# First chunk of a hybrid decoder step: the recurrence-side mixing placed beside the last gates, six half gate units placed behind the first scores, the recurrence placed earlier

## Chip, cores and metric

One core of one Trainium2 chip runs the whole step. The metric is the device time of one execution in microseconds; for a kernel the median of its runs is given.

## What is computed

One layer of a hybrid decoder works on 1024 prompt tokens and 8 sample tokens, with a model width of 1024, in 32-bit floats. The part that matters here, cut from the reference:

```python
proj = rmsnorm(x, norm_mix) @ w_in
u_s5, x_lru, y_lru, g_a, g_b = split(proj)
a_out = s5_branch(u_s5, ...)             # state scan, then z * sigmoid(z @ w_glu + b)
b_out = rglru_branch(x_lru, y_lru, ...)  # conv, gates, scan, times gelu(y_lru)
merged = sigmoid(g_a) * (a_out @ w_proj_a) + sigmoid(g_b) * (b_out @ w_proj_b)
x = x + merged @ w_out
x = x + peer(rmsnorm(x, norm_ffn), w_q, sub_keys, u_tab, v_tab)
```

In `peer`, each token ranks keys for 8 heads and takes the 16 best experts of each. An expert is one row of `u_tab` and one of `v_tab`, so 128 expert rows are gathered for every token, 1024 + 1024 numbers each.

## The kernel before

The prompt is cut into four chunks of 256 tokens, and a chunk into two tiles of 128. The sample tokens ride with the last chunk. Each chunk has a trunk (input projections, state scan, recurrence, gates, mixing, output) and an expert part: for every list position of a tile one gather brings 128 rows, one for each token, 1 MB with both tables. VectorE takes the dot product of the u half with the normed token (line 1824, `dots`), ScalarE turns it into a weight (line 856 is its helper), and TensorE adds the v half, weighted by a diagonal matrix (line 2277, `values`). GpSimd issues the gathers (line 802, `gather`). The trunk of a later chunk runs between the batches of the chunk ahead of it, by due times (`paced`, line 357). The first chunk has no expert work to run beside, so its trunk stands alone, and it is written out by hand so that the first tile's first list is ready soon: `first_lists` on TensorE (line 2345), VectorE (line 1942) and ScalarE (line 990).

In the trunk of the first chunk TensorE goes through units of eight products; a unit has 128 output channels and 256 tokens. Line 2165 is `project`, and a matmul in 32 bits stands as two records in the trace, so a unit is x16. Behind the four recurrence gates come gate units 4 to 15 (`U_GATE` + m). Between them stand the state steps: `s5_in` (line 2182) and `s5_out` (line 2206, with the skip part at line 2194 for every second one). How many of the sixteen steps are done ahead of gate unit m is fixed in a tuple, and the steps are in the order input 0, input 1, output 0, input 2, output 1 and so on:

```python
FIRST_AFTER = (1, 1, 2, 4, 6, 8, 8, 10, 12, 12, 12, 14, 14, 15, 15, 16)
```

So output 3 and input 5 stand ahead of gate unit 7, output 4 and input 6 ahead of unit 8, and output 7 ahead of unit 15. Output j waits for the three VectorE pieces of state pair j (`s5`, line 1559; a scan is line 1581, the last copy of a pair line 1606). Input j + 1 waits for the first two products of pair j, which read PSUM. VectorE's order of pieces is a string: S is a state piece, L is half of one of the four recurrence units (`lru`, line 1609; scan at line 1619); a C does nothing in the first chunk:

```python
FIRST_DVE = "SSSSSCSCSCSCSSSSSS" + "SL" * 8 + "SS"
```

In `first_lists`, TensorE then does the gated unit of the state branch for tile 0 (line 2366), the eight mixing units of tile 0 (line 2321, `mix_side`: four products for side 0, the state branch, and four for side 1, the recurrence), its output (line 2388), transposes (line 2360), the first head's queries (line 2353) and scores (line 2412). While VectorE ranks the first list (`first_topk`, line 1696), TensorE does what is left of the gated units of tile 1, spreads the norm's weights over a bank (line 2243), and begins the mixing of tile 1. This goes on when VectorE has finished the last gated products, in `last_gates`. Behind it come the second head's queries and scores, the output of tile 1 (line 2435) with the first batches of `values` between its units, and the other heads.

VectorE follows: the mixing of a unit takes three operations (`mix`, line 1916), then the residual (line 1314), then the norm. `first_topk` releases the first eight gathers through `best_ok` and the next eight through `idx_ok`. In `upto(OLD + k)` the first k batches of two dots are done. One such batch stands in the middle of tile 1's mixing, two more stand inside the second ranking, and two more between that ranking and the residual of tile 1.

Gathers go round five pairs of cells (15 cells of 4 KB a partition; `u_cell`, `v_cell`), so gather i waits for the dot of row i - 5, and for the v product of row i - 10. Weights come through a ring of two slots that hold a pair of units, or have a home of their own (`HOMES`, line 89): output weights, five mixing weights, the gated units' weights, and three mixing weights parked in cells 13, 14 and 12. A gather that would write a cell in use waits for the units that read it (lines 834 to 839). SyncE loads in the order of use, and waits for a ring slot (`slot_free`, line 682) or, ahead of the output weights, for the recurrence (`lru_ok`). At position 68 of that order it waits for the end of tile 1's mixing, then loads keys and query weights; the next chunk's columns wait for the residual of tile 1.

Of the kernel before, what the change touches and what calls it, by code (L numbers as in the profile page):

```python
# [14 lines left out]
P = 128  # L15
# [53 lines left out]
U_MIX0, U_OUT0, U_Q0, U_MIX1, U_Q01, U_OUT1, U_Q1, UNITS0 = 36, 44, 52, 54, 62, 64, 72, 88  # L69
SLOTS0 = UNITS0 - 4  # L70
TRUNK = 28
EVACS0 = 56
# [15 lines left out]
MIX_CELLS = (13, 14, 12)  # L88
HOMES = RESIDENT + GLU_W + MIX_PARKED
# [31 lines left out]
FIRST_DVE = "SSSSSCSCSCSCSSSSSS" + "SL" * 8 + "SS"  # L121
# [204 lines left out]
def slot_unit(c, l):  # L326

    if c:
        return l if l < L_GATE else l + 8
    return l if l < U_GATE else ga_unit(c, l - U_GATE) if l < TRUNK else l + 4  # L330
# [61 lines left out]
def build(nc, i_, o_):  # L392

    with ExitStack() as ctx:
# [5 lines left out]
        def sem(name):  # L400
# [101 lines left out]
        assert W.at <= T.at + GLU_AT and min(MIX_CELLS) * D >= GLU_AT + QT * DB  # L502
        homes = [R.take(D) for _ in RESIDENT] \
            + [rows_[:, GLU_AT + DB * k:GLU_AT + DB * k + DB] for k in range(QT)] \
            + [cells[:, k] for k in MIX_CELLS]
# [157 lines left out]
        def _(sp):  # L663
# [58 lines left out]
            def first_chunk():  # L722

                for l in range(2 * RING, SLOTS0):
                    if l == 68:
                        sp.wait_ge(unit, U_MIX1 + KT)
                        keys(1, 0)
                    if l == 72:
                        next_columns(0)
                    if l >= 72 and l % 4 == 0:  # L730
                        pair = (l - 64) // 4
                        keys(pair, 2 * (pair - 1) if pair > 2 else 0)
                    if l == U_OUT0 - 4:
                        sp.wait_ge(lru_ok, QT)
                    slot_free(0, l)
                    load_weights(0, l)
                    if l == 47:
                        load_x(0, False)
                        sp.wait_ge(y_mm, SJ // 2)
                        sp.dma_start(kb0, i_["keys"][:, 0:4, :]).then_inc(key0_in, 16)  # L740
# [42 lines left out]
        def _(pool):  # L783
# [39 lines left out]
            def gathers(c, first, last):  # L823

                for i in range(first, last):
# [8 lines left out]
                    if c == 0 and i < UV:  # L834
                        held = {u_cell(i), v_cell(i)}
                        if held & {GLU_AT // D, GLU_AT // D + 1}:
                            pool.wait_ge(glu_mm, 2 * QT)
                        if held & set(MIX_CELLS):
                            pool.wait_ge(unit, U_MIX1 + 1 + max(k for k, cell in enumerate(MIX_CELLS) if cell in held))
                    gather_to(place(c, i), flat(idxn)[:, i:i + 1])  # L840
# [13 lines left out]
        def _(act):  # L854
# [135 lines left out]
            def first_lists(upto):  # L990
# [45 lines left out]
                root(0, 0)  # L1036
                for h, first_unit in enumerate((U_Q0, U_Q01)):
                    if h:
                        for q in range(2, QT):
                            glu(q, QT + q, slice(P, C))  # L1040
                        soft(0, P, 1)
                    for s in range(2):
                        query(first_unit + s, h, s, qT0[:, s])
# [34 lines left out]
            def chunk(c, last):  # L1078
# [56 lines left out]
                def mixing_gate(m):  # L1135
# [7 lines left out]
                    af(dst, PB[u % 2][:, 0:n], ACT.Tanh, scale=0.5).then_inc(evac, 1)  # L1143
# [158 lines left out]
        def _(dve):  # L1302
# [639 lines left out]
            def first_lists(upto):  # L1942
# [31 lines left out]
                for m in range(KT):  # L1974
                    mix(0, m, U_MIX0 + m, early, MIXB[m % 2])
# [16 lines left out]
                scale(0)  # L1992
                for i, m in enumerate(LAST_FIRST):
                    if i == QT:
                        upto(OLD + 1)
                    mix(0, m, U_MIX1 + 4 * (i // 4) + 3, late, [b[:, P * (i % 4):P * (i % 4) + P] for b in MIXB[i // 4]])
                dve.wait_ge(s_ev, 2)
                for piece, _ in enumerate(topk(1, P, 1, lambda t: gn[:, 1], lambda t: idxn[:, 1])):
                    if piece == 1:
                        upto(OLD + 2)  # L2000
                    elif piece == 3:
                        upto(OLD + 3)
# [127 lines left out]
        def _(pe):  # L2130
# [214 lines left out]
            def first_lists(upto):  # L2345

                def query(u, s, cols, evicted):

                    w = slot(0, u - 4)
# [22 lines left out]
                pe.wait_ge(lru_ok, QT)  # L2372
                pe.wait_ge(glu_ev, QT)
                w01 = [slot(0, TRUNK + QT + m) for m in range(2)]
                for m in range(2):
                    mix_side(w01[m], 1, MIXB[m], early)
                pe.wait_ge(a0_ok, QT)
                for m in range(2):
                    mix_side(w01[m], 0, MIXB[m], early).then_inc(unit, 1)
                for m in range(2, KT):  # L2380
                    pe.wait_ge(mix_ok, m - 1)
                    mix(0, TRUNK + QT + m, MIXB[m % 2], early)
# [23 lines left out]
                def head(h, first_unit):  # L2406

                    for s in range(2):
                        query(first_unit + s, s, early, U_MIX0 + 2 * h)
                    pe.wait_ge(evac, U_MIX0 + 2 * h + 2)  # L2410
# [14 lines left out]
                for i in range(KT):  # L2425
                    if i >= QT:
# [4 lines left out]
                for i, k in enumerate(LAST_FIRST):  # L2431
                    pe.wait_ge(mix_ok, KT + i + 1)
                    w = slot(0, U_OUT1 - 4 + k)
# [15 lines left out]
                for h in range(2, HEADS):  # L2449
                    for s in range(2):  # L2450
                        upto(at0_proj(h, s))
                        query(U_Q1 + 2 * (h - 2) + s, s, slice(0, C), U_MIX0 + 2 * h + s - 1)
# [3 lines left out]
                    pe.wait_ge(evac, U_MIX0 + 2 * h + 2)  # L2456
# [10 lines left out]
                for h in range(2):  # L2467
                    for s in range(2):
                        upto(at0_proj(HEADS, 0) + 2 * h + s)
                        query(U_Q1 + 12 + 2 * h + s, s, late, U_MIX0 + 16 + 2 * h + s - 1)  # L2470
# [11 lines left out]
            def chunk(c, last):  # L2482
# [33 lines left out]
                if first:  # L2516
# [201 lines left out]
```

## Time and profile before

| what | value |
|---|---|
| median of 3 runs | 3051.58 us (3050.4 to 3053.53) |
| the profiled execution: time | 3053.22 us |
| the profiled execution: span | 3051.4 us |
| mean granted TensorE clock | 0.866 |
| DMA traffic | 1215.48 MB, 398 GB/s over the span |
| busy share of the span: TensorE, VectorE, ScalarE, GpSimd | 80%, 71%, 40%, 37% |

The span runs from the first to the last instruction of the profiled execution; its time has the launch around it. The shares of the engines are means over stages with different limits: in the first 190 us the gathers have not begun, and in the rest they run all the time. PE is TensorE, DVE VectorE, ACT ScalarE, POOL GpSimd, SP SyncE. A row of a timeline has the start, the length, and in brackets the idle time ahead of it with what ended it.

### The profile page before, as it was taken

What the parts mean: (1) busy time and instruction counts of PE and PEld (TensorE: products, weight loads), DVE (VectorE), ACT (ScalarE), POOL (GpSimd) and SP (SyncE); (2) the same over time, 40 slices, a digit from 0 to 9 for tenths busy, and PEclk for the clock granted to TensorE, in tenths of its full rate; (3) what the DMA queues carried; (4) which work ended last, traced back from release to release, by engine and by line L of the source; (5) the groups of instructions that cost most, each with busy time, mean ns of one, the idle gap of its engine ahead of it and who ended that gap; (6) DMA issues with size and microseconds to landing.
All of it is one profiled execution on the core that took longest, in us unless ns stands there. A gap on an engine that the chain in (4) does not pass through costs nothing.

```text
span 3051.4 us, 43432 instructions
## 1 busy us (share of the span) xinstructions
PE 2442.7 (80%) x14628; PEld 1180.5 (39%) x14628; DVE 2162.8 (71%) x5374; ACT 1207.0 (40%) x3786; POOL 1121.5 (37%) x1048
## 2 busy tenths in 40 slices
PE   9997768899887778899877768888977776766776
PEld 7863324565343324455233324455433321111111
DVE  7757887776479876676468987676558897554445
ACT  2224444433345444333335444433244444333333
POOL 0023443433334443333333443333334444433332
PEclk9998888999988879999988879999988886677667
DMA  4569999999999999999999999999999999999998
GB/s 156 200 242 408 407 411 421 420 417 414 412 420 412 421 420 420 421 404 421 420 421 406 406 419 413 421 419 420 419 414 419 409 416 419 419 421 421 420 421 344
DMA packets 176079, 1215.48 MB, mean 398 GB/s; under 512 B 22360, under 2 KB 22744, under 8 KB 31472
## 3 DMA queue, kind: packets, MB, share of 16 engines
q0 software_dynamic: 148608, 1082.20, 85.9%
q1 hardware_dynamic: 25744, 126.19, 10.4%
q10 hardware_dynamic: 1504, 4.33, 0.4%
q8 instruction: 115, 1.88, 0.3%
q14 instruction: 108, 0.88, 0.1%
HBM read 1208.12 MB, written 4.51 MB: 397 GB/s over the span
## 4 chain that ended last, share of the span: by engine, by line
DMA 29%; issue 22%; PE 20%; DVE 15%; POOL 11%; ACT 2%; DVEq 0%; ACTq 0%; POOLq 0%; SPq 0%
DMA arena<-in_uv,arena 15%; DMA arena<-in_vu,arena 14%; POOL arena L802 11%; PE psum L2277 7%; DVE arena L1824 6%; PE psum L2165 5%; PE psum L2321 3%; DVE arena L1306 3%; ACT arena L856 2%; DVE arena L1314 1%; DVE arena L1687 1%; PE psum L2341 1%; PE psum L2353 1%; DVE arena L1645 1%; DVE arena L1310 0%
## 5 line engine op out<-in xcount | busy, mean ns | idle before, releaser
L1824 DVE CUSTOM_DVE_ANT_0 arena<-arena 128x1024 f32<-128x1024 f32 x1024 | 1246.7, 1224 | 762.5 <-DMA arena<-in_uv,arena 392.4
L2277 PE MATMUL psum<-arena 64*64 64x512 f32 x8184 | 1282.6, 730 | 556.2 <-ACT arena L856 504.4
L856 ACT ACTIVATE arena<-arena 128x1 f32<-128x1 f32 (+3 forms) x3252 | 932.6, 289 | 1630.8 <-DVE arena L1824 1449.6
L802 POOL DMA_INDIRECT arena<-in_vu,arena x517 | 554.5, 1073 | 987.8 <-DVE arena L1824 690.7
L802 POOL DMA_INDIRECT arena<-in_uv,arena x515 | 563.8, 1095 | 920.6 <-DVE arena L1824 810.5
L2277 PEld LDWEIGHTS psum<-arena 64*64 64x64 f32 x8184 | 276.1, 150 | 1370.2 <-ACT arena L856 1102.9
L2165 PE MATMUL psum<-arena 128*128 128x256 f32 (+1 forms) x2656 | 653.7, 403 | 2.8 <-DVE arena L1314 1.7
L2165 PEld LDWEIGHTS psum<-arena 128*128 128x128 f32 x2656 | 519.3, 200 | 201.9 <-issue 122.7
L1306 DVE TENSOR_TENSOR arena<-arena 128x256 f32<-128x256 f32 (+11 forms) x562 | 249.9, 471 | 12.9 <-ACT psum L856 0.8
L856 ACT ACT_TABLE_LOAD x119 | 152.7, 1283 | 10.9 <-DVE arena L1306 7.0
L856 ACT ACTIVATE arena<-psum 128x256 f32<-128x256 f32 (+5 forms) x246 | 95.2, 400 | 108.9 <-PE psum L2165 79.6
L2321 PE MATMUL psum<-arena 128*128 128x128 f32 (+2 forms) x640 | 119.1, 343 | 2.3 <-DVE arena L1314 1.7
L1314 DVE SCALAR_TENSOR_TENSOR arena<-arena 128x256 f32<-128x256 f32 (+8 forms) x287 | 98.1, 354 | 20.6 <-ACT arena L856 15.2
L2321 PEld LDWEIGHTS psum<-arena 128*128 128x128 f32 x640 | 100.0, 191 | 28.5 <-issue 11.2
L2341 PE MATMUL psum<-arena 128*128 128x512 f32 x192 | 88.7, 604 | 0.0
L1824 DVE DVE_READ_ACCUMULATOR2_ANT arena<- 128x1 f32 x1024 | 84.3, 82 | 0.0
L1314 DVE SCALAR_TENSOR_TENSOR arena<-arena,psum 128x128 f32<-128x128 f32 (+4 forms) x101 | 51.2, 544 | 27.0 <-PE psum L2321 21.9
L1581 DVE TENSOR_TENSOR_SCAN arena<-arena 128x64 f32<-128x64 f32 x256 | 68.9, 332 | 1.3
L2353 PE MATMUL psum<-arena 128*128 128x256 f32 (+1 forms) x320 | 64.0, 357 | 0.4 <-issue 0.4
L2353 PEld LDWEIGHTS psum<-arena 128*128 128x128 f32 x320 | 53.3, 202 | 22.8 <-issue 17.9
L1306 DVE TENSOR_TENSOR arena<-psum,arena 128x512 f32<-128x512 f32 (+2 forms) x91 | 59.7, 685 | 1.3 <-PE psum L2277 0.2
L856 ACT ACTIVATE arena<-psum,arena 128x256 f32<-128x256 f32 (+3 forms) x75 | 31.5, 450 | 70.7 <-PE psum L2360 31.2
(139 smaller groups left out, 1048.0 us busy)
## 6 DMA issues: line engine op xcount, KB each, us to landing
arena<-in_w_in SPq DMA_DIRECT2D x56, 1024.0 KB, 9.1
arena<-in_w_q SPq DMA_DIRECT2D x34, 1024.0 KB, 9.6
arena<-in_vu,arena POOLq DMA_INDIRECT x517, 11.3
arena<-in_uv,arena POOLq DMA_INDIRECT x515, 11.3
arena<-in_w_ab SPq DMA_DIRECT2D x11, 512.0 KB, 10.0
arena<-in_keys SPq DMA_DIRECT2D x17, 256.0 KB, 7.7
arena<-in_w_out SPq DMA_DIRECT2D x8, 512.0 KB, 16.0
arena<-in_x_tok SPq DMA_DIRECT2D x8, 512.0 KB
```

The source lines that it names most:

```text
L802: pool.indirect_dma_start(rows_[:, first:first + 2 * D], None, table, bass.IndirectOffsetOnAxis(column, 0)).then_inc(uv_in[at % UV], 16)
L856: return nc.scalar.activation(out, in_, f, **kw)
L1306: return V.tensor_tensor(out, a, b, op)
L1314: return V.scalar_tensor_tensor(out=out, in0=a, scalar=s1, in1=b, op0=op0, op1=op1)
L1581: return V.tensor_tensor_scan(v, mag2[:, j:j + 1].to_broadcast([P, SEG]), v, start, ALU.mult, ALU.add)
L1645: ins = V.match_replace(M[:, k], SV[:, k, best], src[:, k], NEG)
L1824: V.tensor_tensor_reduce(out=u, in0=u, in1=hn, scale=1.0, scalar=0.0, op0=ALU.mult, op1=ALU.add, accum_out=dots_[:, b % DOTS, k:k + 1]).th ...
L2165: ins = mm(PB[u % 2][:, 0:n], w[:, P * t:P * t + P], rhs[:, t, 0:n], start=(t == 0), stop=(t == k - 1))
L2277: ins = mm(PV[o:o + HP, half], dg[r:r + HP, PAIR * (b % 2) + k], cells[r:r + HP, v_cell(place(c, i)), at:at + 512], start=(i % (SLOT // 2) ...
L2321: ins = mm(banks[side][:, 0:cols.stop - cols.start], w[:, 512 * side + P * t:512 * side + P * t + P], src[:, t, cols], start=(t == 0), sto ...
L2341: ins = mm(OUTB[t][half][0:rn], hT[c][:, k, r0:r0 + rn], w[:, 512 * half:512 * half + 512], start=(k == 0), stop=(k == KT - 1))
L2353: ins = mm(PB[s][:, 0:n], w[:, P * t:P * t + P], gb[:, t, cols], start=(t == 0), stop=(t == KT - 1))
```

## The change

Six of the twelve later gate units, numbers 10 to 15, are computed for the first tile alone in the trunk. Their second tile's half comes later, behind the first head's scores, in two banks by turns, and ScalarE evicts it (`late_gate`): two ahead of the first softmax, four behind it. For this the six weights get homes in cells 9, 10, 12, 13, 2 and 5, the parked mixing weights move to cells 14, 11 and 8, and gathers into these cells wait for the late units. The load into cell 2 waits for the state tables that used the place.

The recurrence side of tile 0's eight mixing units goes beside gate units 12 to 15, two units at each, into the two banks called `x2T`; in `first_lists` only the state side is left, into four banks by turns. So TensorE waits for the whole recurrence ahead of the first of them, at gate unit 12, and VectorE's order of pieces has each recurrence unit in one go, the last behind the fourteenth state piece. The two halves of tile 1's mixing swap their banks. VectorE does the first two batches of dots ahead of tile 1's mixing, and none within it. `FIRST_AFTER` stays. The core of the diff:

```diff
...
-U_MIX0, U_OUT0, U_Q0, U_MIX1, U_Q01, U_OUT1, U_Q1, UNITS0 = 36, 44, 52, 54, 62, 64, 72, 88
-SLOTS0 = UNITS0 - 4
+LATE_GATES = (10, 11, 12, 13, 14, 15)
+LATE = len(LATE_GATES)
+U_MIX0, U_OUT0, U_Q0, U_LATE = 36, 44, 52, 54
+U_MIX1, U_Q01, U_OUT1, U_Q1, UNITS0 = (u + LATE for u in (54, 62, 64, 72, 88))
+SLOTS0 = UNITS0 - 4 - LATE
...
-MIX_CELLS = (13, 14, 12)
-HOMES = RESIDENT + GLU_W + MIX_PARKED
+MIX_CELLS = (14, 11, 8)
+LATE_W = tuple(("w_in", U_GATE + m) for m in LATE_GATES)
+LATE_CELLS = (9, 10, 12, 13, 2, 5)
+HOMES = RESIDENT + GLU_W + MIX_PARKED + LATE_W
...
-FIRST_DVE = "SSSSSCSCSCSCSSSSSS" + "SL" * 8 + "SS"
+FIRST_DVE = "S" * 10 + "SLL" * 4 + "S" * 10
...
+                    if weight(0, l) == LATE_W[4]:
+                        sp.wait_ge(s5_ok, 1)
...
+                        elif held & set(LATE_CELLS):
+                            pool.wait_ge(unit, U_LATE + 1 + max(k for k, cell in enumerate(LATE_CELLS) if cell in held))
...
+                def late_gate(i):
+                    act.wait_ge(unit, U_LATE + i + 1)
+                    af(gb[:, LATE_GATES[i] % KT, P:C], SB[i % 2][:, 0:P], ACT.Tanh, scale=0.5).then_inc(evac, 1)
+
...
+                        for i in range(2):
+                            late_gate(i)
...
+                        for i in range(2, LATE):
+                            late_gate(i)
...
-                    af(dst, PB[u % 2][:, 0:n], ACT.Tanh, scale=0.5).then_inc(evac, 1)
+                    k = P if first and m in LATE_GATES else n
+                    af(dst[:, 0:k], PB[u % 2][:, 0:k], ACT.Tanh, scale=0.5).then_inc(evac, 1)
...
-                    mix(0, m, U_MIX0 + m, early, MIXB[m % 2])
+                    mix(0, m, U_MIX0 + m, early, (GLUB[m % 4], x2T[:, P * m:P * m + P]))
...
+                dve.wait_ge(hn_ok, 1)
+                upto(OLD + 2)
+                dve.wait_ge(evac, U_MIX0 + 2 + LATE)
...
-                    if i == QT:
-                        upto(OLD + 1)
-                    mix(0, m, U_MIX1 + 4 * (i // 4) + 3, late, [b[:, P * (i % 4):P * (i % 4) + P] for b in MIXB[i // 4]])
+                    mix(0, m, U_MIX1 + 4 * (i // 4) + 3, late, [b[:, P * (i % 4):P * (i % 4) + P] for b in MIXB[1 - i // 4]])
...
-                        upto(OLD + 2)
+                        upto(OLD + 3)
...
-                        upto(OLD + 3)
+                        upto(OLD + 4)
...
-                pe.wait_ge(lru_ok, QT)
...
-                w01 = [slot(0, TRUNK + QT + m) for m in range(2)]
-                for m in range(2):
-                    mix_side(w01[m], 1, MIXB[m], early)
...
-                for m in range(2):
-                    mix_side(w01[m], 0, MIXB[m], early).then_inc(unit, 1)
-                for m in range(2, KT):
-                    pe.wait_ge(mix_ok, m - 1)
-                    mix(0, TRUNK + QT + m, MIXB[m % 2], early)
+                for m in range(KT):
+                    if m >= QT:
+                        pe.wait_ge(mix_ok, m - QT + 1)
+                    mix_side(slot(0, TRUNK + QT + m), 0, (GLUB[m % 4], None), early).then_inc(unit, 1)
...
+                pe.wait_ge(glu_ev, QT + 2)
+                for i, m in enumerate(LATE_GATES):
+                    w = slot(0, U_GATE + m)
+                    if i >= 2:
+                        pe.wait_ge(evac, U_MIX0 + 1 + i)
+                    for t in range(KT):
+                        ins = mm(SB[i % 2][:, 0:P], w[:, P * t:P * t + P], hT[0][:, t, late], start=(t == 0), stop=(t == KT - 1))
+                    ins.then_inc(unit, 1)
...
-                places = [[b[:, P * (i % 4):P * (i % 4) + P] for b in MIXB[i // 4]] for i in range(KT)]
-                w1 = [slot(0, U_MIX1 - 4 + m) for m in LAST_FIRST]
+                places = [[b[:, P * (i % 4):P * (i % 4) + P] for b in MIXB[1 - i // 4]] for i in range(KT)]
+                w1 = [slot(0, U_MIX1 - 4 - LATE + m) for m in LAST_FIRST]
...
+                    if i == QT:
+                        pe.wait_ge(evac, U_MIX0 + 2 + LATE)
...
-                        project(c, ga_unit(c, m), U_GATE + m, hT[c], KT, n)
+                        project(c, ga_unit(c, m), U_GATE + m, hT[c], KT, P if m in LATE_GATES else n)
+                        if m >= EARLY_SIDES:
+                            if m == EARLY_SIDES:
+                                pe.wait_ge(lru_ok, QT)
+                            for k in range(2 * (m - EARLY_SIDES), 2 * (m - EARLY_SIDES) + 2):
+                                mix_side(slot(c, TRUNK + QT + k), 1, (None, x2T[:, P * k:P * k + P]), slice(0, P))
...
```

What is left out of the diff renumbers units, evictions and waits by the six new units, and gives the new cells their place in the list of homes.

## Rows read from the trace of the kernel before

**Rows 1.** The page: gigabytes a second in 40 equal slices, and the gather queue.

```profile
GB/s 156 200 242 408 407 411 421 420 417 414 412 420 412 421 420 420 421 404 421 420 421 406 406 419 413 421 419 420 419 414 419 409 416 419 419 421 421 420 421 344
q0 software_dynamic: 148608, 1082.20, 85.9%
```

**Rows 2.** Windows by stage: us, busy by engine, granted clock, DMA share, GB/s.

```profile
90.00:189.00 99.00, 96.28 (x671) 79.73 (x668) 59.67 (x204) 17.30 (x40) 0.32 (x1) 1.00 0.46 173
190.00:230.00 40.00, 38.33 (x242) 23.25 (x244) 30.35 (x90) 14.62 (x42) 15.63 (x14) 1.00 0.99 401
230.00:265.00 35.00, 29.25 (x172) 16.72 (x164) 23.84 (x78) 17.66 (x48) 11.06 (x10) 0.91 1.01 419
265.00:280.00 15.00, 12.90 (x68) 6.21 (x69) 14.69 (x45) 6.19 (x21) 7.56 (x6) 0.74 0.95 360
```

**Rows 3.** Timeline of GpSimd, gathers 1, 5 and 16: start us, us, what.

```profile
188.68 1.09 POOL L802 DMA_INDIRECT arena<-in_vu,arena  x1 [184.83 <-DVEq L1752]
193.86 0.94 POOL L802 DMA_INDIRECT arena<-in_vu,arena  x1 [0.30 <-issue]
232.14 1.68 POOL L802 DMA_INDIRECT arena<-in_uv,arena  x1 [4.84 <-DVE arena L1824]
```

**Rows 4.** Chain of waits on TensorE to the first gather: start us, us, what.

```profile
98.50 1.00 PE psum L2206 x16
99.50 1.09 PE psum L2182 x16
100.59 3.65 PE psum L2165 x16
104.24 0.57 PE psum L2194 x16
106.90 10.56 PE psum L2165 x48
...
147.86 10.99 PE psum L2321 x96
```

**Rows 5.** Timeline of VectorE, state pieces and the first recurrence unit.

```profile
96.06 1.28 DVE L1306 TENSOR_TENSOR arena<-psum,arena 128x512 f32<-128x512 f32 x2
...
103.21 0.76 DVE L1314 SCALAR_TENSOR_TENSOR arena<-arena 128x256 f32<-128x256 f32 x2
103.88 1.28 DVE L1306 TENSOR_TENSOR arena<-psum,arena 128x512 f32<-128x512 f32 x2
...
105.88 0.42 DVE L1314 SCALAR_TENSOR_TENSOR arena<-arena 128x256 f32<-128x256 f32 x1
...
107.52 1.07 DVE L1581 TENSOR_TENSOR_SCAN arena<-arena 128x64 f32<-128x64 f32 x4
```

**Rows 6.** TensorE's timeline and windows of 1 us where its clock fell and rose.

```profile
259.86 3.69 PE L2277 MATMUL psum<-arena 64*64 64x512 f32 x16 [3.83 <-ACT arena L856]
300.19 3.51 PE L2277 MATMUL psum<-arena 64*64 64x512 f32 x16 [2.13 <-ACT arena L856]
...
259.00:260.00 1.00, 0.14 (x4) 0.14 (x8) 1.00 (x4) 0.70 (x4) 0.94 (x1) 0.51 0.96 401
303.00:304.00 1.00, 1.00 (x10) 0.35 (x3) 0.81 (x2) 0.00 (x0) 0.00 (x0) 0.80 1.06 442
```

**Rows 7.** Timeline of TensorE behind the first head's scores.

```profile
183.95 3.74 PE L2321 MATMUL psum<-arena 128*128 128x128 f32 x32
189.42 10.98 PE L2321 MATMUL psum<-arena 128*128 128x128 f32 x96 [1.74 <-DVE arena L1314]
```

**Rows 8.** Timelines of VectorE (residual, eleventh row's dot, third ranking) and ScalarE (its scores).

```profile
226.45 1.29 DVE L1314 SCALAR_TENSOR_TENSOR arena<-psum,arena 128x512 f32<-128x512 f32 x2 [0.66 <-PE psum L2435]
230.64 1.23 DVE L1824 CUSTOM_DVE_ANT_0 arena<-arena 128x1024 f32<-128x1024 f32 x1 [0.16 <-issue]
251.23 0.87 DVE L1642 MAX8 arena<-arena 128x8 f32<-128x128 f32 x4
...
244.79 0.82 ACT L856 ACTIVATE arena<-psum,arena 128x256 f32<-128x256 f32 x2
```

More of the change, by code:

```diff
@@ L67 @@
 EVACS = 56
-U_MIX0, U_OUT0, U_Q0, U_MIX1, U_Q01, U_OUT1, U_Q1, UNITS0 = 36, 44, 52, 54, 62, 64, 72, 88
-SLOTS0 = UNITS0 - 4
+LATE_GATES = (10, 11, 12, 13, 14, 15)
[3 more added lines that the diff above has]
+SLOTS0 = UNITS0 - 4 - LATE
 TRUNK = 28
-EVACS0 = 56
+EVACS0 = 56 + LATE
+EARLY_SIDES = 2 * KT - KT // 2
 LAST_FIRST = (5, 6, 7, 0, 1, 2, 3, 4)
@@ L329, in slot_unit @@
         return l if l < L_GATE else l + 8
-    return l if l < U_GATE else ga_unit(c, l - U_GATE) if l < TRUNK else l + 4
+    return l if l < U_GATE else ga_unit(c, l - U_GATE) if l < TRUNK else l + 4 if l < U_LATE - 4 else l + 4 + LATE
 def columns(c):
@@ L501, in build @@
         GLU_AT = 6 * D
-        assert W.at <= T.at + GLU_AT and min(MIX_CELLS) * D >= GLU_AT + QT * DB
+        assert W.at <= T.at + GLU_AT and min(MIX_CELLS + LATE_CELLS[:4]) * D >= GLU_AT + QT * DB
         homes = [R.take(D) for _ in RESIDENT] \
             + [rows_[:, GLU_AT + DB * k:GLU_AT + DB * k + DB] for k in range(QT)] \
-            + [cells[:, k] for k in MIX_CELLS]
+            + [cells[:, k] for k in MIX_CELLS + LATE_CELLS]
         dg = R.take(2 * PAIR, HP)
@@ L2347, in query @@
                 def query(u, s, cols, evicted):
-                    w = slot(0, u - 4)
+                    w = slot(0, u - 4 if u < U_LATE else u - 4 - LATE)
                     pe.wait_ge(evac, evicted)
@@ L2406, in head @@
                 def head(h, first_unit):
+                    evicted = U_MIX0 + (2 + LATE) * h
                     for s in range(2):
-                        query(first_unit + s, s, early, U_MIX0 + 2 * h)
-                    pe.wait_ge(evac, U_MIX0 + 2 * h + 2)
+                        query(first_unit + s, s, early, evicted)
+                    pe.wait_ge(evac, evicted + 2)
                     for s in range(2):
@@ L2432, in first_lists @@
                     pe.wait_ge(mix_ok, KT + i + 1)
-                    w = slot(0, U_OUT1 - 4 + k)
+                    w = slot(0, U_OUT1 - 4 - LATE + k)
                     for half in range(2):
@@ L2451, in first_lists @@
                         upto(at0_proj(h, s))
-                        query(U_Q1 + 2 * (h - 2) + s, s, slice(0, C), U_MIX0 + 2 * h + s - 1)
+                        query(U_Q1 + 2 * (h - 2) + s, s, slice(0, C), U_MIX0 + LATE + 2 * h + s - 1)
                     if h == 5:
@@ L2455, in first_lists @@
                     upto(at0_scores(h))
-                    pe.wait_ge(evac, U_MIX0 + 2 * h + 2)
+                    pe.wait_ge(evac, U_MIX0 + LATE + 2 * h + 2)
                     pe.wait_ge(key_in[h // 2 % 2], 16 * ((h // 2 - 1) // 2 + 1))
@@ L2469, in first_lists @@
                         upto(at0_proj(HEADS, 0) + 2 * h + s)
-                        query(U_Q1 + 12 + 2 * h + s, s, late, U_MIX0 + 16 + 2 * h + s - 1)
+                        query(U_Q1 + 12 + 2 * h + s, s, late, U_MIX0 + LATE + 16 + 2 * h + s - 1)
                 upto(at0_scores(HEADS))
```

## Prediction, made before the changed kernel was run

> **What bounds the kernel.** I read the page's slices first. From the fourth slice on, the DMA engines move about 420 GB/s to the end, and one queue, the gathers of expert rows, carries 1082 MB of it [rows 1]. The windows by stage say the same: 173 GB/s before the first gather, 419 behind it [rows 2]. So the end is set by three things: when the stream of gathers starts, how many bytes follow, and where the stream runs dry. The bytes stay the same here. Everything this change does is in the first 270 us, and it counts only if it moves the first gather, issued at 188.68 [rows 3], or makes a hole behind it.
>
> In the chain of waits, TensorE leads to the first gather: it is busy for 96 of 99 us at full clock [rows 2], through gate units, state steps, the first tile's mixing and its output [rows 4]. VectorE is as full over the state pieces: from 96.06 to 107.52 its rows follow one another without a gap [rows 5]. That second engine is what one must not lose sight of.
>
> **Shorter gates (removed from the path).** A gate unit of 256 columns takes 10.56/3 = 3.52 on TensorE; eight products of 128 columns, with their weights, take 10.99/6 = 1.83, the time of a mixing unit [rows 4]. Six units cut to their first tile give 6 x 1.69 = 10.1 us.
>
> **The recurrence side of the first mixing (moved).** 32 products leave the stage behind the gates and come in beside the last four gates; by the same row that is 7.3 us out and 7.3 us in, so nothing. The mixing stage keeps the other 7.3 us. What it loses in waits is nothing either, since TensorE had none there.
>
> **The recurrence (moved up).** The order of VectorE becomes ten state pieces, then four times one piece and a whole recurrence unit (two halves), then ten pieces. A unit costs 103.21 to 103.88 and 105.88 to 107.52 [rows 5], 0.67 + 1.64 = 2.31. Back to back, the second half also waits for the first half's writes, which a state piece hides today; between 0 and 0.2 us, I take 0.04, so 2.35. The work is the same, but every state piece behind is late by the units ahead of it until the units are done, and TensorE's program keeps its fixed places for the state steps. Step by step: state output 3, at 98.50 [rows 4], needs the piece that ended as the next began, at 96.06 [rows 5]; one unit later is 98.41. No wait. State input 5, at 99.50 [rows 4], needs the first products of the next piece, ready at 97.34 [rows 5], two units later: 102.04. Wait 2.5. The input's 1.09 and a gate's 3.65 and 0.57 [rows 4] bring TensorE to 107.4. State output 4 needs the piece that ended as the recurrence began, at 103.21 [rows 5], now behind four units: 112.6. Wait 5.2. State input 6 needs 1.28 more of VectorE [rows 5] while the output takes 1.00 [rows 4]: wait 0.3.
>
> So the three gates that began at 106.90 [rows 4] begin 8.0 us later. From there VectorE runs unbroken again and TensorE is behind it, so no wait is left. A small wait for the gated branch, today hidden partly by the recurrence side, grows by some 0.3 us.
>
> **The clock.** A wait of 3.83 on TensorE was followed by a granted clock of 0.51, that is 1.2 instead of 2.4 GHz; after work began at 300.19 the clock was back late in the window from 303, which reads 0.80 [rows 6]. A wait of 1.74 left it at 1.00 [rows 2, 7]. The 5.2 here is longer than the first, so I count 3.2 us of work at half clock: 1.6 lost, between 0 (the clock stays) and 2.6 (as long at half clock as the wait itself). The Trainium skill, "TensorE: Matmul & The Clock Gate", Part 1, says that the throttled state is the default and that activity releases it. By that rule read strictly the wait of 2.5 would cost its 1.6 as well, and the first gather would come at +1.4; by the row that kept its clock over 1.74 it comes at -0.2.
>
> Sum to the first gather: -10.1 + 8.0 + 0.3 + 1.6 = -0.2, bounds -1.8 and +0.8. Ten microseconds of saved work are mostly spent in waiting for pieces that the recurrence has pushed back.
>
> **Weights kept for later.** Six half-megabyte loads go to cells of their own instead of the ring, so the queue of SyncE passes them earlier, with the mixing and output weights behind them; the wait on the state tables is long over at that point. The load windows before the first gather are half empty (DMA share 0.46 [rows 2]). Cost nothing; if that cover went, a late mixing weight would stop TensorE. On GpSimd's queue the fourth and fifth gathers now wait for late units. By the sums below these end at 187.6 and 191.3, and the fifth gather goes out at 193.86 [rows 3], everything behind it later still. Nothing.
>
> **The six second halves (added behind the first scores).** Today TensorE has from 183.95 a recurrence side of 3.74 us, then 1.74 us of waiting, then 10.98 us of second-tile mixing, to 200.4 [rows 7]. Now 6 x 1.83 = 11.0 us come in ahead and swallow the wait: 9.2 us later, 209.6. ScalarE's six short evictions stand beside the first ranking, four of them queued behind its softmax, which itself now stands behind the first two; TensorE's fifth half waits for the third eviction, which follows the softmax and is over by then. If the softmax came late, the second tile would be late with it, by as much. From here on TensorE is without a break up to the second tile's output, so the residual, at 226.45, and the dot that waits behind it on VectorE, at 230.64 [rows 8], both come 9.2 us later, whatever the four dots moved ahead of the mixing bring: the program has the same ten dots before that residual as today.
>
> A gather can start only when the dot of the row five before it is done. So the sixteenth gather goes from 232.14 [rows 3] to 241.3. Would the queues be dry by then? By shapes, fifteen rows (1.05 MB each), two pairs of query weights, the next columns (1.05 MB each) and two key blocks (0.26) are 19.4 MB. From 190 to 230, 401 GB/s moved 16.0 [rows 2]; the other 3.4 MB last 8.0 us, to 238.0. A gather's data moves 1.3 to 3 us behind its issue (188.68, and 1.7 us missing in that window against 419 GB/s); I take 2. Slack: 238.0 - 2 - 232.14 = 3.9. A hole of 9.2 - 3.9 = 5.3 us.
>
> Some comes back. The third ranking, at 251.23, stands behind its rows today, not behind its scores; these are out at 245.61 [rows 8], 254.8 after. VectorE is then 3.6 late, the stream 5.3, and from 265 to 280 the stream is short of dots today (share 0.95, 360 GB/s [rows 2]). Between 0 and 1.7 us; I take 1.0.
>
> **Sum.** -0.2 + 5.3 - 1.0 = +4.1 us. The profiled execution has a span of 3051.4 and a time of 3053.22, 1.6 above the median; its time would be 3057.3, and the median 3051.58 becomes 3055.7. 0.2%, about what a measurement here can tell from no change, is 6.1 us: the forecast is no change, on the slow side.
>
> **Rivals.** First, slower: the hole takes the whole delay. At the second tile's residual, VectorE waits for TensorE with its rows landed. If the early dots let the stream eat its backlog sooner, or smaller holes open between the dots inside the second ranking, then all 9.2 us are dry, with the start at its worst, +0.8: +10.0, 3061.6. It decides once the backlog at the sixteenth gather is below 3.9 us. For it: only nine rows can be asked for before the second ranking begins. Against: the weight loads, also late, fill in between. 0.22.
>
> Second, a little faster: the clock stays and the ramp is covered. That is -1.8 and a hole of nothing: 3049.8. For it: four dots come ahead of the mixing and ask for four rows sooner, and the late weight loads fill in. Against: the count of bytes, in which both already stand. 0.14.
>
> Third, faster: the change does what its words say and TensorE does not wait for the state pieces. Then the first gather comes 9.8 earlier, the ramp's 4.3 stays: -5.5, 3046.1. It needs state steps that are not due at those places; the chain shows TensorE arriving at output 3 with 2.4 to spare and no more. 0.06.
>
> **How the numbers follow.** The forecast has 0.58; its own range is 3051.5 to 3060, from the bounds of clock, hole and return. The range 3048.8 to 3062 takes in the second rival and the slower one's middle. Slower by over 0.2%: nearly all of the first rival and about an eighth of the forecast, 0.28. Faster: over half of the last rival and a little for what I have not seen, 0.05. Same: 0.67.
>
> **What would show it.** In the changed trace: the recurrence's last write near 110; TensorE idle by 2.5 and 5.2 us before state input 5 and output 4; a granted clock below 1 near 113 to 118; the first mixing's end near 159; the first gather between 187 and 190; the second tile's mixing ending 9 us later against the first gather; a dip of DMA in the windows near 236 to 243. The forecast is wrong if the first gather comes before 185, or if the DMA share stays at 1.00 through 245, or if the sixteenth gather is less than 6 us later.

## The result, and the profile after

The median of 19 runs is 3057.88 us, against 3051.58 for 19 runs of the kernel before beside them. The ratio is 1.0017 with a 95% interval of [1.0011, 1.0024], so the kernel is 5.2 us slower (0.0017 x 3051.58), between 3.4 and 7.3. The medians lie 6.3 apart and the means 5.3, since the runs of after spread over 7.8 us and those of before over 3.8. By the 0.2% of the prediction (6.1 us) this is no change, on the slow side, though the upper end of the interval lies above it. The profiled execution of after took 3058.52 with a span of 3056.7. Its span is 5.3 above the one of before, 3051.4.

The page of after, gigabytes a second in 40 slices and the gather queue:

```profile
GB/s 155 237 191 388 415 413 415 421 416 414 416 421 412 413 420 421 421 409 421 420 420 409 412 420 405 421 420 420 418 415 417 403 420 420 420 421 422 421 420 344
q0 software_dynamic: 148608, 1082.20, 85.7%
```

Packets and bytes are those of [rows 1]. The third and fourth slices are thinner, 191 for 242 and 388 for 408; from there on the two kernels look alike. So the difference was made in the first 310 us. Windows by stage (busy time by engine, granted clock, DMA share, GB/s):

```profile
90.00:189.00 99.00, 91.14 (x676) 76.23 (x672) 59.25 (x198) 16.96 (x40) 0.00 (x0) 0.95 0.45 173
190.00:230.00 40.00, 38.33 (x276) 29.70 (x275) 28.24 (x88) 12.69 (x38) 13.45 (x13) 1.00 0.94 368
230.00:265.00 35.00, 34.53 (x203) 18.88 (x201) 20.51 (x64) 15.12 (x45) 11.27 (x10) 1.00 0.95 362
265.00:280.00 15.00, 9.61 (x55) 4.33 (x52) 14.61 (x40) 8.33 (x25) 6.51 (x5) 0.77 1.01 416
```

Against [rows 2], TensorE is busy for 91 instead of 96 of the 99 us before the first gather, at a mean clock of 0.95. From 190 to 265 the stream moved 14.7 + 12.7 = 27.4 MB where before it moved 16.0 + 14.7 = 30.7: 3.3 MB less, 7.9 us at 419 GB/s. From 265 to 280 it is the other way: 416 for 360 GB/s, 0.84 MB or 2.0 us given back.

Gathers 1, 6, 15 and 16 on GpSimd's timeline (start us, us, what, idle before):

```profile
190.28 1.09 POOL L810 DMA_INDIRECT arena<-in_vu,arena  x1 [186.43 <-DVEq L1771]
...
198.28 0.94 POOL L810 DMA_INDIRECT arena<-in_uv,arena  x1 [1.89 <-DVE arena L1843]
...
234.99 0.94 POOL L810 DMA_INDIRECT arena<-in_vu,arena  x1 [2.75 <-PE psum L2297]
242.46 1.68 POOL L810 DMA_INDIRECT arena<-in_uv,arena  x1 [6.53 <-DVE arena L1843]
```

Against [rows 3] the start is 1.6 late and the sixteenth gather 10.3, so 8.7 us of delay were added between them. TensorE's timeline shows both parts:

```profile
98.83 1.07 PE L2226 MATMUL psum<-arena 128*32 128x128 f32 x16
102.46 1.17 PE L2202 MATMUL psum<-arena 32*128 32x128 f32 x16 [2.56 <-DVE arena L1325]
103.56 5.35 PE L2185 MATMUL psum<-arena 128*128 128x256 f32 x16
...
113.05 1.33 PE L2226 MATMUL psum<-arena 128*32 128x128 f32 x16 [3.57 <-DVE arena L1625]
114.31 2.08 PE L2202 MATMUL psum<-arena 32*128 32x128 f32 x16
116.31 11.03 PE L2185 MATMUL psum<-arena 128*128 128x256 f32 x48
...
153.07 7.38 PE L2341 MATMUL psum<-arena 128*128 128x128 f32 x64 [0.83 <-ACT arena L866]
160.29 13.90 PE L2403 MATMUL psum<-arena 128*128 128x512 f32 x32
...
185.55 10.88 PE L2441 MATMUL psum<-arena 128*128 128x128 f32 x96
196.27 14.46 PE L2341 MATMUL psum<-arena 128*128 128x128 f32 x128
```

State input 5 waits 2.56 us for VectorE and state output 4 another 3.57; gate unit 7 between them takes 5.35 instead of 3.65 [rows 4]. Near the end stand the six late halves, 10.88 us, and behind them the second tile's mixing without a break. Why unit 7 is slow, the windows of 1 us say (the clock is the third number from the end):

```profile
103.00:104.00 1.00, 1.00 (x13) 0.87 (x10) 0.97 (x4) 0.00 (x0) 0.00 (x0) 0.74 1.03 414
104.00:105.00 1.00, 1.00 (x3) 0.73 (x3) 0.96 (x2) 0.00 (x0) 0.00 (x0) 0.50 1.02 414
...
106.00:107.00 1.00, 1.00 (x4) 0.81 (x3) 0.93 (x6) 0.00 (x0) 0.00 (x0) 0.56 1.02 418
107.00:108.00 1.00, 1.00 (x6) 0.88 (x5) 0.96 (x6) 0.00 (x0) 0.00 (x0) 1.00 1.01 412
...
114.00:115.00 1.00, 1.00 (x10) 0.70 (x8) 0.94 (x3) 0.00 (x0) 0.00 (x0) 0.50 1.01 401
...
120.00:121.00 1.00, 1.00 (x5) 0.86 (x4) 1.00 (x3) 0.00 (x0) 0.00 (x0) 0.73 1.05 418
```

The granted clock fell to 0.50 (1.2 GHz) behind each of the two waits and came back to 1.00 within the windows from 106 and from 120. VectorE, from the last recurrence unit to the third ranking:

```profile
108.21 1.20 DVE L1333 SCALAR_TENSOR_TENSOR arena<-arena 128x256 f32<-128x256 f32 x3
...
112.83 0.17 DVE L1625 COPY arena<-arena 128x4 f32<-128x4 f32 x1
...
236.77 1.29 DVE L1333 SCALAR_TENSOR_TENSOR arena<-psum,arena 128x512 f32<-128x512 f32 x2 [5.33 <-PE psum L2461]
240.96 1.23 DVE L1843 CUSTOM_DVE_ANT_0 arena<-arena 128x1024 f32<-128x1024 f32 x1 [0.16 <-issue]
...
256.91 1.23 DVE L1843 CUSTOM_DVE_ANT_0 arena<-arena 128x1024 f32<-128x1024 f32 x1 [2.49 <-DMA arena<-in_uv,arena]
258.06 0.87 DVE L1661 MAX8 arena<-arena 128x8 f32<-128x128 f32 x4
```

The copy at 112.83 ends the piece that state output 4 wants. The residual and the eleventh dot are 10.3 late against [rows 8], with VectorE idle for 5.33 ahead of the residual. The dot at 256.91 waits for its row, and the third ranking stands right behind it, 6.8 late.

### The profile page after: what moved, and what is told of

The parts are those of the page before. It is cut to its first block, busy times and chain, and to the rows that moved or that the text cites. A ratio compares the mean times of both kernels' runs of the same rounds, so it can differ in the third digit from the quotient of the medians.

```text
span 3056.7 us, 43640 instructions
## 1 busy us (share of the span) xinstructions
PE 2432.9 (80%) x14724; PEld 1173.2 (38%) x14724; DVE 2162.7 (71%) x5374; ACT 1206.8 (39%) x3792; POOL 1125.1 (37%) x1048
## 4 chain that ended last, share of the span: by engine, by line
DMA 31%; issue 21%; PE 20%; DVE 14%; POOL 10%; ACT 3%; ACTq 0%; DVEq 0%; POOLq 0%; SPq 0%
DMA arena<-in_uv,arena 17%; DMA arena<-in_vu,arena 14%; POOL arena L810 10%; PE psum L2297 9%; DVE arena L1843 6%; PE psum L2185 4%; DVE arena L1325 3%; PE psum L2341 3%; ACT arena L866 2%; DVE arena L1333 1%; PE psum L2361 1%; DVE arena L1706 1%; DVE arena L1600 1%; PE psum L2373 0%; PE psum L2403 0%
## 5 line engine op out<-in xcount | busy, mean ns | idle before, releaser
L2185 PE MATMUL psum<-arena 128*128 128x256 f32 (+2 forms) x2656 | 636.4, 396 | 3.7 <-DVE arena L1333 1.8
L2185 PEld LDWEIGHTS psum<-arena 128*128 128x128 f32 x2656 | 507.2, 198 | 198.2 <-issue 122.5
L2341 PEld LDWEIGHTS psum<-arena 128*128 128x128 f32 x640 | 100.1, 190 | 26.7 <-issue 13.0
L2373 PE MATMUL psum<-arena 128*128 128x256 f32 (+1 forms) x320 | 61.0, 345 | 0.4 <-issue 0.4
L2373 PEld LDWEIGHTS psum<-arena 128*128 128x128 f32 x320 | 50.8, 193 | 21.5 <-issue 17.1
L2361 PEld LDWEIGHTS psum<-arena 128*128 128x128 f32 x192 | 36.0, 197 | 56.8 <-issue 56.8
```

The lines of the kernel that those rows point to most:

```text
L2185: ins = mm(PB[u % 2][:, 0:n], w[:, P * t:P * t + P], rhs[:, t, 0:n], start=(t == 0), stop=(t == k - 1))
L2341: ins = mm(banks[side][:, 0:cols.stop - cols.start], w[:, 512 * side + P * t:512 * side + P * t + P], src[:, t, cols], start=(t == 0), sto ...
L2361: ins = mm(OUTB[t][half][0:rn], hT[c][:, k, r0:r0 + rn], w[:, 512 * half:512 * half + 512], start=(k == 0), stop=(k == KT - 1))
L2373: ins = mm(PB[s][:, 0:n], w[:, P * t:P * t + P], gb[:, t, cols], start=(t == 0), stop=(t == KT - 1))
```

## The experiments

All eight are edits of the changed kernel, in two groups on two chips (e1 to e4, e5 to e8), each with its own runs of the kernel before beside it (median 3052.14 of 33 runs for the first group, 3052.47 of 21 for the second). The ratios are taken against these, so between groups the ratios and the gathers can be compared, and the medians can't. The time differences in the text are these ratios applied to 3051.58; where two edits are compared, it is by their ratios.

| kernel | first gather | sixteenth gather | median us | ratio to before [95%] |
|---|---|---|---|---|
| before | 188.68 | 232.14 | 3051.58 | 1 |
| after | 190.28 | 242.46 | 3057.88 | 1.0017 [1.0011, 1.0024] |
| e1_steps | 179.51 | 231.70 | 3048.39 | 0.9985 [0.9976, 0.9994] |
| e2_filler | 186.90 | 239.10 | 3054.56 | 1.0008 [0.9999, 1.0017] |
| e3_dots | 190.12 | 236.09 | 3055.99 | 1.0012 [1.0003, 1.0021] |
| e4_order | 187.23 | 239.42 | 3056.14 | 1.0013 [1.0004, 1.0022] |
| e5_steps_dots | 179.66 | 225.63 | 3045.08 | 0.9976 [0.9966, 0.9986] |
| e6_steps_whole | 198.78 | 242.25 | 3061.92 | 1.0030 [1.0018, 1.0042] |
| e7_steps_three | 186.41 | 233.24 | 3049.36 | 0.9988 [0.9979, 0.9997] |
| e8_old_dots | 190.58 | 242.77 | 3062.24 | 1.0033 [1.0020, 1.0045] |

**e1_steps: the state steps put where VectorE can serve them.** Each entry of the tuple says how many of the sixteen steps are done ahead of a gate unit; lower entries are later steps. The last step goes behind the gates.

```diff
-FIRST_AFTER = (1, 1, 2, 4, 6, 8, 8, 10, 12, 12, 12, 14, 14, 15, 15, 16)
+FIRST_AFTER = (1, 1, 2, 4, 6, 8, 8, 9, 10, 10, 10, 12, 12, 14, 14, 15)
...
-                if not first:
+                if first:
+                    first_s5(2 * (SJ // 2))
+                else:
                     s5_until(AT_GLU)
```

> The changed kernel with the state steps that TensorE waits for issued later among the gate units (input 5 behind gate unit 7, output 4 and input 6 behind unit 10, the last output behind unit 15). My theory: the early recurrence costs only because these steps keep their places. TensorE then has no wait above 1 us between 98 and 150, its clock stays at 1.00, the first mixing ends near 149 and the first gather goes out near 179 instead of 190.3; the hole behind it stays, so the time is some 10 us below the changed kernel: about 3047 us, 3044 to 3050. Rival, that VectorE's state pieces bound the stage whatever TensorE's order: the first gather stays at 187 or later and the time above 3054.

TensorE's timeline, from state output 3 on:

```profile
98.47 1.07 PE L2226 MATMUL psum<-arena 128*32 128x128 f32 x16
99.47 3.72 PE L2185 MATMUL psum<-arena 128*128 128x256 f32 x16
103.11 1.16 PE L2202 MATMUL psum<-arena 32*128 32x128 f32 x16
104.20 8.96 PE L2185 MATMUL psum<-arena 128*128 128x256 f32 x48
...
149.53 10.90 PE L2403 MATMUL psum<-arena 128*128 128x512 f32 x25
```

A gate unit now stands where the wait of 2.56 was, and the three units that took 11.03 take 8.96. The first mixing ends at 149.53 instead of 160.29, where the output begins (this view ends at 160, so its last row is cut short). The first gather goes out at 179.51, 9.2 earlier than before the change and 10.8 earlier than after it. So the waits came from the fixed places of the steps, and the saving of 10.1 us of gates is real once they go; VectorE was not the bound. The time is 9.8 below after, as expected. Against before it falls by 4.6, though, half of the 9.2: the sixteenth gather is only 0.4 earlier than before, so 8.7 of the 9.2 are gone there, as in after, and part of them comes back later.

**e2_filler: idle products in the two waits.** The waits stay; products of ones into a bank that nobody reads keep TensorE busy in them.

```diff
+                if c == 0 and jp == 5:
+                    for _ in range(5):
+                        mm(PV[:, 1, 0:C], ones, ones[:, 0:1].to_broadcast([P, C]), start=True, stop=True)
...
+                if c == 0 and jp == 4:
+                    for _ in range(11):
+                        mm(PV[:, 1, 0:C], ones, ones[:, 0:1].to_broadcast([P, C]), start=True, stop=True)
```

> The changed kernel with idle products into a free bank in the two waits of TensorE (5 of 256 columns ahead of state input 5, 11 ahead of state output 4), so that it waits busily. My theory: the fall of the granted clock alone costs about 3 us here, two times 1.5. Granted clock 1.00 from 100 to 125, gate unit 8 begins near 113.5 instead of 116.3, the first gather near 187, time 3 us below the changed kernel. Rival, that the clock costs nothing since VectorE's pieces bound the stage: first gather 189.5 to 191, time the same within 1 us.

Its timeline of TensorE:

```profile
99.51 2.44 PE L2193 MATMUL psum<-arena 128*128 128x256 f32 x10
102.14 1.16 PE L2205 MATMUL psum<-arena 32*128 32x128 f32 x16 [0.19 <-DVE arena L1325]
103.23 3.72 PE L2185 MATMUL psum<-arena 128*128 128x256 f32 x16
...
107.45 5.05 PE L2221 MATMUL psum<-arena 128*128 128x256 f32 x22
112.73 1.07 PE L2232 MATMUL psum<-arena 128*32 128x128 f32 x16 [0.22 <-DVE arena L1625]
113.92 1.16 PE L2205 MATMUL psum<-arena 32*128 32x128 f32 x16
115.01 8.96 PE L2185 MATMUL psum<-arena 128*128 128x256 f32 x48
```

State output 4 comes at 112.73, near the 112.6 of the prediction, because VectorE sets it; unit 7 takes 3.72, the three units 8.96, and the clock reads 1.00 from 90 to 189. The first gather is 3.4 us earlier than in after. Of this, 0.3 has nothing to do with the waits: in the profiled execution of after gate unit 4 already began that much later (84.80, here 84.49). So the clock is 3.1, and of the 10.8 us by which e1 starts sooner than after, 0.3 is that shift, 3.1 the clock and 7.4 the waits themselves. The time is lower by 2.7 (0.0009), with intervals that overlap; what shows the clock's cost is the timeline.

**e3_dots: one more batch of dots ahead of the residual's wait.**

```diff
-                upto(OLD + 5)
+                upto(OLD + 6)
                 dve.wait_ge(unit, U_OUT1 + KT)
                 residual(0, 1, P, PB)
```

> The changed kernel with the batch of the eleventh and twelfth dot ahead of the second tile's residual on VectorE instead of behind it. My theory: the hole in the gather stream comes from VectorE standing at that residual with landed rows. The sixteenth gather goes out near 233 instead of 242.5, the DMA share from 230 to 250 rises, and the time falls by 2 to 4 us, to about 3054. Rival, that the hole is made inside the second ranking or by the late weight loads: time the same within 1 us.

Gathers 15 to 18:

```profile
234.84 0.95 POOL L810 DMA_INDIRECT arena<-in_vu,arena  x1 [2.75 <-DVE arena L1843]
236.09 0.94 POOL L810 DMA_INDIRECT arena<-in_uv,arena  x1 [0.30 <-issue]
238.43 0.94 POOL L810 DMA_INDIRECT arena<-in_uv,arena  x1 [1.40 <-PE psum L2297]
243.34 1.68 POOL L810 DMA_INDIRECT arena<-in_uv,arena  x1 [3.98 <-DVE arena L1843]
```

The sixteenth gather moves up 6.4, to 236.09 instead of the 233 I had expected, but the eighteenth now waits 3.98 for dots behind the same residual. The ratio is lower by 0.0005, 1.5 us, and the intervals overlap. The direction is that of the forecast, the size is not, and in the time the effect isn't shown. The residual's wait on TensorE stays, and the batch moves only two gathers past it. And the sixteenth can't go ahead of the fifteenth, which stands at 234.84 as in after (234.99): it needs the v product of row 5, and TensorE has that batch of `values` from 232.71 to 234.66.

**e4_order: VectorE's order of pieces as it was,** all else as in after.

```diff
-FIRST_DVE = "S" * 10 + "SLL" * 4 + "S" * 10
+FIRST_DVE = "SSSSSCSCSCSCSSSSSS" + "SL" * 8 + "SS"
```

> The changed kernel with VectorE's old order of pieces (the recurrence halves between state pieces, the last behind the twenty-second). My theory: TensorE no longer waits at state input 5 and output 4, but some 6 to 7 us at gate unit 12 for the recurrence, with one fall of the clock instead of two; first gather between 185 and 188.5, time 2 to 4 us below the changed kernel. Rival, that the early recurrence is what makes the recurrence side beside the gates possible: first gather later than 190 and the time above the changed kernel.

```profile
117.84 3.84 PE L2185 MATMUL psum<-arena 128*128 128x128 f32 x32
128.42 3.52 PE L2341 MATMUL psum<-arena 128*128 128x128 f32 x16 [6.74 <-DVE arena L1325]
```

On TensorE's timeline, the waits at the state steps are gone and one of 6.74 stands at gate unit 12, where the recurrence side needs the whole recurrence; the first side behind it runs at half clock (3.52 for 1.95). The first gather comes at 187.23, 3.1 earlier than in after. So with these fixed steps, moving the recurrence up only took TensorE's wait from gate unit 12 to the state steps and split it in two, with a fall of the clock behind each. That cost 3.1 us of start. In the time it shows as 0.0004 or 1.2 us, less than I expected and within the intervals.

**e5_steps_dots: e1 and e3 together.** Both diffs above.

> The changed kernel with both edits: the state steps later, and the batch of the eleventh and twelfth dot ahead of the second tile's residual. My theory, start and hole are separate terms: first gather near 179.5 as with the steps alone, sixteenth gather near 225.5 instead of 231.7, and time 2 us below the steps alone, 3044.5 to 3047.5. Rival, that with an earlier start the hole is set elsewhere: time the same as the steps alone, 3048 to 3049.5.

The ratio is 0.9976 [0.9966, 0.9986]: 7.3 us faster than before, 12.5 faster than after, the lowest ratio here. Its first gather is that of e1, its sixteenth 6.1 earlier than e1's. At the gathers the two terms add: the extra batch moves the sixteenth by 6.1 here and by 6.4 in e3. In the time it is 2.7 us here (0.0009) and 1.5 there, both times with overlapping intervals.

**e6_steps_whole: e1 with no late halves.** The six gates are computed whole in the trunk, their weights back in the ring.

```diff
-LATE_GATES = (10, 11, 12, 13, 14, 15)
+LATE_GATES = ()
-LATE_CELLS = (9, 10, 12, 13, 2, 5)
+LATE_CELLS = ()
...
```

> The state steps later, and no late halves: all gate units whole in the trunk, as before. What is left of the change is the recurrence side beside the gates, the early recurrence and the early dots. My theory, the six halves make the hole: first gather near 189.6 (179.5 and 10.1), sixteenth gather within 1 us of 44 behind it as in the kernel before, no hole, and time 0.9 above the kernel before, as the start says: 3051 to 3054. Rival, that the moved dots or the swapped banks make the hole: the sixteenth gather 52 us behind the first as in the changed kernel, and time 3055.5 or more.

TensorE at gate unit 12:

```profile
117.61 7.17 PE L2185 MATMUL psum<-arena 128*128 128x256 f32 x32
130.94 3.76 PE L2341 MATMUL psum<-arena 128*128 128x128 f32 x16 [6.16 <-DMA arena<-in_w_ab]
```

The sixteenth gather comes 43.47 us behind the first, as before (43.46), and the time is what the start explains within its interval (+9.2 for +10.1). So the hole is the late halves'. But the start was missed by 9.2: a mixing weight came 6.16 us late, and the first side ran at half clock. So the six weights in cells of their own do a second job: they let the mixing weights be loaded early enough for the sides that now run beside the gates.

**e7_steps_three: e1 with three late halves.**

```diff
-LATE_GATES = (10, 11, 12, 13, 14, 15)
+LATE_GATES = (13, 14, 15)
-LATE_CELLS = (9, 10, 12, 13, 2, 5)
+LATE_CELLS = (9, 10, 12)
...
```

> The state steps later, and three late halves (units 13, 14, 15) instead of six. My theory, the ramp has some 5.6 us of room on TensorE (1.74 of waiting and 3.9 of backlog in the stream) and three halves of 1.83 just fit: first gather near 184.6, sixteenth gather near 232, time as the start says, 4 to 4.5 below the kernel before, 3046.5 to 3049. Rival, that every half costs in the ramp what it saves at the start, or half of it: time 3049.5 to 3052.

TensorE at gate unit 12, and the windows of the ramp, in which the stream starts up:

```profile
125.93 2.34 PE L2341 MATMUL psum<-arena 128*128 128x128 f32 x16 [1.19 <-DMA arena<-in_w_ab]
```

```profile
190.00:230.00 40.00, 38.33 (x241) 23.80 (x241) 27.62 (x81) 13.05 (x38) 13.34 (x13) 1.00 1.01 411
230.00:265.00 35.00, 29.85 (x188) 17.50 (x190) 27.86 (x85) 20.23 (x58) 13.36 (x12) 0.94 1.01 408
```

The DMA share stays at 1.01, although the sixteenth gather stands 46.8 us behind the first instead of 43.5: three halves fit into the ramp. The time is 3.7 below before (0.9 to 6.4) for a start 2.3 earlier. The start itself is 186.41 where I expected 184.6, again with a wait for a mixing weight, 1.19.

**e8_old_dots: the batches of dots back in their old places,** behind or within tile 1's mixing.

```diff
-                dve.wait_ge(hn_ok, 1)
-                upto(OLD + 2)
                 dve.wait_ge(evac, U_MIX0 + 2 + LATE)
                 for i, m in enumerate(LAST_FIRST):
+                    if i == QT:
+                        dve.wait_ge(hn_ok, 1)
+                        upto(OLD + 1)
...
-                        upto(OLD + 3)
+                        upto(OLD + 2)
...
-                        upto(OLD + 4)
+                        upto(OLD + 3)
```

> The changed kernel with the dots in their old places (one batch in the middle of the second tile's mixing, one each inside the second ranking, two behind it). My theory: the early batch moves no bytes when the stream is full and the count of dots ahead of the residual is the same, so first gather 190.3, sixteenth gather 242 to 243, time the same as the changed kernel within 1.5 us, 3056 to 3059. Rival one, that the early dots ease the ramp: 2 us or more above the changed kernel. Rival two, that they make the hole by holding VectorE: 2 us or more below it.

Gather 6, and the window behind the first gather:

```profile
208.88 1.17 POOL L810 DMA_INDIRECT arena<-in_uv,arena  x1 [12.19 <-DVE arena L1843]
```

```profile
190.00:230.00 40.00, 38.33 (x278) 29.82 (x277) 25.65 (x86) 11.57 (x32) 11.51 (x11) 1.00 0.81 303
```

The sixteenth gather is where it was, but the sixth goes out at 208.88 instead of 198.28. The dot it waits for now stands in the middle of the mixing, which the late halves delay; the stream runs dry in the ramp, at 303 instead of 368 GB/s. The kernel is 10.1 slower than before, 4.9 more than after, with two intervals that overlap at their ends. The dry stretch, 2.6 MB or 6.2 us of the stream at 419 GB/s, is clear. So my expectation that the early dots are worth nothing fell, and the first rival was right: they hide some 5 us that the late halves would otherwise cost.

## Why the prediction was right or wrong

**The sign and size: right, in part by luck.** +4.1 was forecast, +5.2 measured, and the median of 3057.88 lies in the forecast's range of 3051.5 to 3060. The start, the hole (how long the stream of gathers goes short behind the start) and the return (what of it comes back later) were all put too low, by 1.8, 1.0 and 1.6. The error of the return cancels over half of the other two: 1.6 + 6.3 - 2.6 = 5.3 in the profiled execution.

**Waits: right.** State input 5 waited 2.56 for 2.5 forecast. State output 4 began at 113.05 for 112.6, of which some 0.3 was there before: gate unit 4 already began 0.3 late in this execution. State input 6 had no wait for 0.3 forecast, since output 4 ahead of it ran at half clock; in e2, at full clock, it begins 1.19 behind output 4, for 1.00 in [rows 4]. e1, e2 and e4 show the cause: with the steps moved, or the recurrence in its old place, the waits are gone, and with TensorE kept busy VectorE still sets 112.73.

**The clock: the mis-sized term.** "3.2 us of work at half clock: 1.6 lost", bound 2.6. Behind the second wait, three gates took 11.03 for 8.96, an input 2.08 for 1.16 and an output 1.33 for 1.07: 3.25 us lost. At the first gather it is 3.1 in e2. The prediction had taken the length of half clock from [rows 6], 300.19 into the window from 303 (not late in it, as it says: with 0.50 and 1.00 for the two levels, a mean of 0.80 puts the rise at 303.4; the 3.2 us fit that). The trace of the kernel before also had a longer stretch, which it left out:

```profile
267.10 3.69 PE L2277 MATMUL psum<-arena 64*64 64x512 f32 x16 [3.56 <-ACT arena L856]
...
272.00:273.00 1.00, 1.00 (x4) 0.79 (x4) 1.00 (x4) 0.77 (x3) 1.00 (x1) 0.66 1.00 377
```

There TensorE worked for some 5.6 us at half clock, from 267.10 into the window from 272, which alone would lose 2.8, more than the bound. In after it held from 113 into the window from 120. So the start came at +1.6, outside the bound of +0.8: -0.2, plus 1.65 for the clock (3.25 for 1.6), plus 0.45 for state output 4, less the 0.3 of state input 6.

The wait of 2.5, which the prediction let pass without a fall, was followed by a clock of 0.50, too. Here the strict reading of the Trainium skill, "TensorE: Matmul & The Clock Gate", Part 1, forecast the fall that came. That its +1.4 is near the +1.6 is luck: it charged the first gather 1.6 for this fall, and the fall cost it nothing. Unit 7's 1.6 us at half clock (5.35 for 3.72 in e2) were swallowed by the second wait, which shrank from 5.2 to 3.57, since VectorE set its end.

**Late halves: right.** 10.88 us for 11.0; residual, eleventh dot and sixteenth gather all 10.3 late, that is 1.6 + 8.7 for 9.2. e6 shows that they make the hole.

**The hole: 6.3 for 5.3.** The stream is short by 7.9 us up to 265, less the 1.6 of the start. The step that failed is that it counted only bytes up to the sixteenth gather. From 220 to 230 the stream is at 354 GB/s and from 230 to 240 at 329, so smaller holes open earlier. Some are between the dots of the second ranking, as the first rival said. Another is at the fifteenth gather, and no text had it: its dot was done by 231.5, but it waited until 234.99 for TensorE's `values`. These stand between the output units of tile 1, so the late halves delay them too, and earlier dots alone don't help there.

**The early dots: costed wrongly at nothing.** "Whatever the four dots moved ahead of the mixing bring" holds for the residual alone, not for the stream. The prediction named them in favour of its second rival and set them at nothing, by the count of bytes. With the dots in their old places (e8) the time comes out at 3062.24, near the first rival's 3061.6, though by a dry stretch inside the ramp which that rival did not describe. So the forecast came out near because of a cover that is in the change and that I had not priced.

**The return: 2.6 for 1.0,** bound 1.7. The deficit of 7.9 us is 5.3 at the end of the span; 2.0 of it comes back between 265 and 280, and where the other 0.6 does is open. The prediction let the third ranking wait for its scores, at 254.8. It stands at 258.06 behind its rows, as before, and is 6.8 late where the stream is 7.9.

**Weights kept for later: costed at nothing, rightly, but not worthless.** The cover named there, a late mixing weight, is what stopped TensorE in e6 for 6.16 us.

Left open: three late halves with the mixing weights loaded sooner and the extra batch of dots, which e5 and e7 suggest, wasn't tried. Nor is the spread of after's runs explained. It is 7.8 us over 19 runs, and 2.3 over 11 with the waits filled (e2). But e3, which keeps both waits, has 8.0 over 11 runs, e8, which keeps them too, 4.2 over 6, and the kernel before, which has neither, 8.7 over the 33 runs beside e1 to e4. That the waits or the clock make it isn't shown.

## What to carry to other kernels

Work cut from a full engine pays only when the places at which it waits for the next engine move too: 10.1 us of gates came to nothing with the tuple left as it was, and to 9.2 of start with another. Work that is put off "behind" a stage is paid where the next stage feeds a stream: three late halves left the DMA share at 1.01 here, six made a hole of 6.3 us. So count what the stream has been asked for when the late work starts, and let what asks for more (here the dots) go ahead of it. A wait on TensorE can cost more than its own length, by the half clock behind it (3.1 us here behind 3.57), unless the slow work lies in front of another wait, as it did behind the 2.56.

## What was not expected of the hardware

A wait of 2.56 us on TensorE was enough for a granted clock of 0.50 behind it; one of 1.74 was not [rows 2, 7]. Behind 3.57 us the half clock held for some 7 us, from 113 into the window from 120. Idle products in the waits kept it at 1.00 and brought the first gather 3.1 us forward. Work at half clock ahead of another engine's wait cost nothing: gate unit 7's 1.6 us went into the second wait.
